# Branch B of a hybrid decoder layer: which marks free its buffers, and two buffers for each recurrent gate

## The reference, cut to what matters

```python
u = conv_b + sum(xpad[:, j:j + T] * conv_w[j] for j in range(CONV_W))
r = sigmoid(blockdiag(u, ga_w) + ga_b)
ig = sigmoid(blockdiag(u, gx_w) + gx_b)
log_a = -LRU_C * r * softplus(-lam)
a = exp(log_a)
bterm = sqrt(-expm1(2 * log_a)) * (ig * u)
hs = scan(h[t] = a[t] * h[t-1] + bterm[t])
y = hs * silu(z)
return y, hs[:, -1], xpad[:, T:]
```

## Time and profile before

| | us |
|---|---|
| runs shown | 1821.83, 1827.86, 1829.33 (median 1827.86) |
| profiled execution, its own time | 1816.9 |
| its span | 1815.1 |
| TensorE busy | 1612.6 (89% of the span) |
| VectorE busy | 913.3 (50%) |
| ScalarE busy | 563.0 (31%) |
| GpSimd busy | 471.7 (26%) |
| stretch of branch B | about 1386 to 1542 of the span |
| stretch of the last stage | 1542 to 1815 |

### The profile page before, as it was taken

One profiled execution on the slowest core, in us unless ns is written; L12 is line 12 of the kernel. 1 busy time (PEld: TensorE's weight loads), 2 busy tenths in 40 slices (PEclk: granted clock), 3 DMA queues, 4 the chain that ended last, 5 costly groups with the idle time before them and its releaser, 6 DMA issues. The chain is left out here.

```text
span 1815.1 us, 30544 instructions
## 1 busy us (share of the span) xinstructions
PE 1612.6 (89%) x11996; PEld 1418.7 (78%) x11996; DVE 913.3 (50%) x1504; ACT 563.0 (31%) x1111; POOL 471.7 (26%) x461
## 2 busy tenths in 40 slices
PE   7899988888886899999989898888899886999697
PEld 3789965666665788887878898888899875999697
DVE  1660456666551222332224258758873465478576
ACT  0312135544441322222212243625442574001100
POOL 2021101000012111211020366757662130234400
PEclk9899999999998999999999999999999998999899
DMA  9311120000004444334240401202132010644321
GB/s 306 129 48 48 25 83 1 1 1 1 1 2 117 118 131 121 110 106 109 83 139 21 153 24 36 72 25 72 30 104 84 22 52 1 207 152 156 107 101 64
DMA packets 162433, 143.48 MB, mean 79 GB/s; under 512 B 50902, under 2 KB 152306, under 8 KB 161394
## 3 DMA queue, kind: packets, MB, share of 16 engines
q1 hardware_dynamic: 153298, 127.79, 23.4%
q10 hardware_dynamic: 8992, 13.74, 2.2%
HBM read 116.21 MB, written 29.40 MB: 80 GB/s over the span
## 5 line engine op out<-in xcount | busy, mean ns | idle before, releaser
L1009 PE MATMUL ps<-w_hi,h_hi 128*128 128x256 f32 x792 | 228.6, 289 | 19.0 <-DVE h_lo L2522 13.6
L1009 PE MATMUL ps<-w_lo,h_hi 128*128 128x256 f32 x792 | 224.0, 283 | 0.0
L1009 PE MATMUL ps<-w_hi,h_lo 128*128 128x256 f32 x792 | 223.8, 283 | 0.0
L1009 PE MATMUL ps<-h_hi,w_hi 128*128 128x344 f32 x648 | 215.7, 333 | 8.9 <-DVE aq L2364 3.5
L1009 PE MATMUL ps<-h_lo,w_hi 128*128 128x344 f32 x648 | 209.4, 323 | 0.0
L1009 PE MATMUL ps<-h_hi,w_lo 128*128 128x344 f32 x648 | 209.0, 323 | 0.0
L1009 PEld LDWEIGHTS ps<-w_hi,h_hi 128*128 128x128 f32 x792 | 151.0, 191 | 21.1 <-issue 14.5
L1009 PE MATMUL ps<-h_hi,wg_hi 128*128 128x344 f32 x432 | 146.1, 338 | 14.0 <-ACT gate_stage L1780 13.1
L900 POOL CAST w_hi<-w_raw 128x1024 fp32r<-128x1024 f32 (+1 forms) x50 | 53.5, 1070 | 387.0 <-DMA w_raw<-in_w_in 163.3
L1009 PEld LDWEIGHTS ps<-w_lo,h_hi 128*128 128x128 f32 x792 | 151.1, 191 | 0.0
L1009 PEld LDWEIGHTS ps<-w_hi,h_lo 128*128 128x128 f32 x792 | 151.0, 191 | 0.0
(11 more groups left out here) (437 smaller groups left out, 3549.1 us busy)
## 6 DMA issues: line engine op xcount, KB each, us to landing
w_raw<-in_w_in SPq DMA_DIRECT2D x46, 512.0 KB, 4.9
sgm<-gate_spill SPq DMA_DIRECT2D x22, 516.0 KB, 6.0
gate_spill<-gate_stage ACTq DMA_DIRECT2D x54, 172.0 KB, 2.4
w_raw<-in_w_in SPq DMA_DIRECT2D x34, 256.0 KB, 4.3
adw<-in_ada_w SPq DMA_DIRECT2D x8, 1024.0 KB, 11.3
pgc<-in_cache_nsa_kv SPq DMA_DIRECT2D x128, 64.0 KB, 2.4
pg<-in_cache_nsa_kv SPq DMA_DIRECT2D x64, 128.0 KB
w_raw<-in_w_branch SPq DMA_DIRECT2D x12, 512.0 KB, 4.4
```

The source lines that it names most:

```text
L1009: last = mm(out, lhsT=l, rhs=r, start=(i == 0 and j == 0), stop=(i == n - 1 and j == 2))
```

## The change

- BR and BI get two buffers each (BR of the even blocks lies where a branch A buffer was, which is also the place of SGM[0] of the merge gates).
- ScalarE waits with BXP for u_ready (the convolution of two blocks before) instead of b_done; with the gate tiles for b_done of two blocks before; a new mark b_scan, given by the scan, frees BA and BT, and ScalarE waits for it before the exponential; BZ now waits for b_done of two blocks before, and so does SGM[0] at j = 4.
- OCO gets four columns, one for each block. The two copies from BXP go to the start of `b_conv`; the two from BHS come right after the scan.
- y is made in BZ instead of BA.

```diff
--- before.py
+++ after.py
@@ -459,13 +459,13 @@
     BXP = sb("bxp", o_, [2, 8 + 3 + T]); o_ += 2 * 1040
     BZ = sb("bz", o_, [2, TC]); o_ += 2 * TC
     BU = sb("bu", o_, [2, TC]); o_ += 2 * TC
-    BR = sb("br", o_, [TC]); o_ += TC
-    BI = sb("bi", o_, [TC]); o_ += TC
+    BR = [sb("br_even", O_CS, [TC]), sb("br_odd", o_, [TC])]; o_ += TC
+    BI = [sb("bi%d" % i, o_ + TC * i, [TC]) for i in range(2)]; o_ += 2 * TC
     BA = sb("ba", o_, [TC]); o_ += TC
     BT = sb("bt", o_, [TC]); o_ += TC
     BHS = sb("bhs", o_, [TC]); o_ += TC
     GWB = sb("gwb", o_, [2, 2, P]); o_ += 512
-    OCO = sb("oco", o_, [2, 32]); o_ += 64
+    OCO = sb("oco", o_, [4, 32]); o_ += 128
     OCR = sb("ocr", o_, [4, P], parts=32); o_ += 512
     assert o_ <= END, o_ - END
 
@@ -1563,7 +1563,7 @@
         def columns_out(j):
 
             pe.wait_ge(e("oc_cols"), j + 1)
-            nc.tensor.transpose(ps[0:20, 6, P * j:P * j + P], OCO[:, j % 2, 0:20], ID).then_inc(e("oc_rows"), 1)
+            nc.tensor.transpose(ps[0:20, 6, P * j:P * j + P], OCO[:, j, 0:20], ID).then_inc(e("oc_rows"), 1)
 
         for j in range(5):
             if j < 4:
@@ -1974,7 +1974,7 @@
                         if j == 0:
                             act.wait_ge(e("a_free"), 4)
                         if j >= 2:
-                            act.wait_ge(e("b_done"), j - 1)
+                            act.wait_ge(e("u_ready"), j - 1)
 
                         st(A(BXP[:, j % 2, 0:8], ps[:, b, 0:8], CP))
                         st(A(BXP[:, j % 2, 11:3 + CH], ps[:, b, 8:CH], CP), act3.free)
@@ -1983,18 +1983,21 @@
                 st.mark(e("bx_ready"))
             if j:
                 jj = j - 1
-                if jj:
-                    act.wait_ge(e("b_done"), jj)
-                for x, dst in ((0, BR), (1, BI)):
+                gr = BR[jj % 2]
+                if jj >= 2:
+                    act.wait_ge(e("b_done"), jj - 1)
+                for x, dst in ((0, gr), (1, BI[jj % 2])):
                     for c in range(3):
                         b = ta.take(act)
                         st(A(dst[:, CH * c:CH * c + CH], ps[:, 3 + b, 0:CH], ACT.Sigmoid, bias=PRM[:, 48 + 4 * x + jj:49 + 4 * x + jj]), ta.free)
 
-                st(A(BA, BR, ACT.Exp, scale=C8[:, jj:jj + 1]))
-                st(A(BT, BR, ACT.Tanh, scale=C8[:, 4 + jj:5 + jj]))
-
-                st(A(BR, BT, ACT.Ln, bias=1.0))
-                st(A(BR, BR, ACT.Exp, scale=-1.0), e("b_at"))
+                if jj:
+                    act.wait_ge(e("b_scan"), jj)
+                st(A(BA, gr, ACT.Exp, scale=C8[:, jj:jj + 1]))
+                st(A(BT, gr, ACT.Tanh, scale=C8[:, 4 + jj:5 + jj]))
+
+                st(A(gr, BT, ACT.Ln, bias=1.0))
+                st(A(gr, gr, ACT.Exp, scale=-1.0), e("b_at"))
 
             def b_gate(x):
                 for c in range(3):
@@ -2002,15 +2005,18 @@
                     st(A(SGM[x][:, CH * c:CH * c + CH], ps[:, b, 0:CH], ACT.Tanh, scale=0.5), act3.free)
 
             if j == 4:
+                act.wait_ge(e("b_done"), 3)
                 b_gate(0)
             if j < 4:
+                if j >= 2:
+                    act.wait_ge(e("b_done"), j - 1)
                 for c in range(3):
                     b = act3.take(act)
                     st(A(BZ[:, j % 2, CH * c:CH * c + CH], ps[:, b, 0:CH], CP), act3.free)
             if j:
                 act.wait_ge(e("b_om"), jj + 1)
                 st(A(BT, BT, ACT.Sqrt, scale=2.0))
-                st(A(BR, BZ[:, jj % 2, :], ACT.Sigmoid), e("b_sq"))
+                st(A(gr, BZ[:, jj % 2, :], ACT.Sigmoid), e("b_sq"))
             if j == 4:
                 b_gate(1)
 
@@ -2452,6 +2458,8 @@
             cb = PRM[:, 44 + j:45 + j]
             v.wait_ge(e("bx_ready"), j + 1)
             xp, us, up = BXP[:, s, 8:11 + T], BU[:, s, 0:NS], BU[:, s, NS:TC]
+            st(cp(OCO[:, j, 0:8], BXP[:, s, 0:8]))
+            st(cp(OCO[:, j, 8:11], BXP[:, s, 8 + T:11 + T]))
             st(ts(up, xp[:, 0:T], cw[0], cb, MUL, ADD))
             for i in (1, 2, 3):
                 st(stt(up, in0=xp[:, i:i + T], scalar=cw[i], in1=up, op0=MUL, op1=ADD))
@@ -2468,23 +2476,21 @@
             s = j % 2
             v.wait_ge(e("b_at"), j + 1)
 
-            st(tt(BT, BT, BR, MUL), e("b_om"))
-            st(tt(BI, BI, BU[:, s], MUL))
+            gr, gi, y = BR[s], BI[s], BZ[:, s]
+            st(tt(BT, BT, gr, MUL), e("b_om"))
+            st(tt(gi, gi, BU[:, s], MUL))
             st(tt(BHS[:, 0:NS], BA[:, 0:NS], CST[:, j, 24:32], MUL))
             v.wait_ge(e("b_sq"), j + 1)
-            st(tt(BI, BI, BT, MUL))
-            st(tt(BHS[:, 0:NS], BHS[:, 0:NS], BI[:, 0:NS], ADD))
-            st(V.tensor_tensor_scan(BHS[:, NS:TC], BA[:, NS:TC], BI[:, NS:TC], 0.0, MUL, ADD))
-            st(tt(BZ[:, s], BZ[:, s], BR, MUL))
-            st(tt(BA, BHS, BZ[:, s], MUL))
-            st(cp(YH[0][:, j], BA))
-            st(tt(YH[1][:, j], BA, YH[0][:, j].bitcast(F32), SUB))
-
-            oc = OCO[:, s]
-            st(cp(oc[:, 0:8], BXP[:, s, 0:8]))
-            st(cp(oc[:, 8:11], BXP[:, s, 8 + T:11 + T]))
+            st(tt(gi, gi, BT, MUL))
+            st(tt(BHS[:, 0:NS], BHS[:, 0:NS], gi[:, 0:NS], ADD))
+            st(V.tensor_tensor_scan(BHS[:, NS:TC], BA[:, NS:TC], gi[:, NS:TC], 0.0, MUL, ADD), e("b_scan"))
+            oc = OCO[:, j]
             st(cp(oc[:, 11:12], BHS[:, TC - 1:TC]))
             st(cp(oc[:, 12:20], BHS[:, 0:8]))
+            st(tt(y, y, gr, MUL))
+            st(tt(y, BHS, y, MUL))
+            st(cp(YH[0][:, j], y))
+            st(tt(YH[1][:, j], y, YH[0][:, j].bitcast(F32), SUB))
             if j:
                 b_rows(j - 1)
             st.mark(e("oc_cols"))
```

## The result

| | runs | median us | lowest to highest |
|---|---|---|---|
| before | 4 | 1828.59 | 1821.83 to 1829.56 |
| changed | 4 | 1807.60 | 1799.90 to 1812.99 |

The changed kernel takes 0.9891 of the time before (95% interval 0.9856 to 0.9925), 19.9 us less by the ratio and 21.0 us less by the medians. The forecast was 1806.9 us.

What follows compares the result with a forecast made beforehand. TensorE bound it, idling in branch B because b_done released several buffers together. Between 19.0 and 22.4 us won, 21 was taken off the median 1827.86, giving 1806.9 us, range 1798 to 1819.

Steps and rivals of the forecast that it cites:

- Second set: Branch B gate products, j=2: ScalarE reads banks directly, six products take about 3.3 us; 5.3 us won.
- New wait for weights: TensorE before x3: weights loaded behind b_done and split by GpSimd are ready at 1458.5, a wait of about 1 us.
- Third set: Gate products, j=3: the set takes 3.3 us, z3 begins at 1473.3 against 1481.59; 8.3 us won so far.
- Fourth set: Gate products, j=4: TensorE's wait falls from 15.11 to 3.9 us; BG begins at 1492.7, or 1494.2 at half clock.
- The scan: VectorE before ScalarE's exponential at j=4: b_scan at 1494.3, with ScalarE then waiting for TensorE at BG's last bank.
- The y products: End of branch B: y products begin at 1519.9 instead of 1542.26, 22.4 us earlier; 19.0 at the low end.
- mishap: Half clock after the fourth wait, 2.3 us together, or GpSimd holding BT*gr, 1.1 us on the path; one taken, not both.
- y in z's place: Recurrence tail: with the four-column OCO it changes no duration, so nothing beyond the 0.41 us from the copies.
- rival 2: Last stage, 1650 to 1700 us: its idleness grows and gives back 14.4 us, leaving 6.6 us won, 1821; chance 0.08.
- Rival 1: ScalarE-VectorE ring over single BA, BT, BHS still binds if GpSimd holds fall on it: 9.4 us lost, 1816; chance 0.10.
- rival 3: Kernel slower: chip grants half clock in dense stretches; 60 us of it gives 1867, 31 us gives 1838; chance 0.04.
- 4: The rival that something else in ScalarE's order holds the fourth set: at most 8.3 us won, 1819.5; chance 0.05.

Runs made afterwards that it cites:

- e9: e7's kernel with the last stage's first split once its buffer is free, the second after oc_done; 106.60 us from first gate set to first y product.
- e4: Changed kernel with ScalarE waiting for b_done instead of b_scan before the exponential; 114.33 us from first gate set to first y product, against 108.77.
- e1: Changed kernel with both old b_done waits back, for x and gate banks; 128.14 us from first gate set to first y product, run of 1833.47.
- e7: Changed kernel with the edits of e5 and e6, and unit BG loaded early too; 106.62 us from first gate set to first y product.
- e10: Changed kernel with GpSimd waiting in branch A for x_ready of the same head before its long operations; 1794.77 us, 0.9826 of before.
- e12: Kernel before with only the branch A wait of e10; 1816.64 us, 0.9931 of the kernel before.
- e6: Changed kernel with GpSimd waiting for block 2's b_scan before splitting the last stage's first weights; 112.08 us from first gate set to first y product.
- e2: Changed kernel with only x waiting for b_done again; 114.27 us from first gate set to first y product, against 108.77.
- e3: Changed kernel with only the gate banks waiting for b_done of the block just before; 123.96 us from first gate set to first y product.
- e5: Changed kernel with the fourth x group's weights loaded ahead of SyncE's wait; 106.99 us from first gate set to first y product, against 108.77.
- e8: e7's kernel with 27 matmuls of the first y products made during TensorE's wait; 376.1 us from first gate set to end, run of 1799.50.
- e11: Edits of e9 and e10 with the partial products of e8; 1790.21 us, 0.9789 of the kernel before.

## Why the prediction was right, point by point

I put the changed kernel's times back by the 12.95 us of branch A, so that they stand on the prediction's clock. x3 is the x group of block 3, z2 the z group of block 2.

- **Second set.** Forecast: z2 begins at 1445.4. Measured 1458.27-12.95 = 1445.3. Right to a tenth, including that six products with ScalarE beside them take 3.2 us.
- **New wait for weights.** Forecast about 1 us, x3 at 1458.6. Measured 1.73 us between records and 2.0 from z2's transpose, x3 at 1459.2. GpSimd's second subtraction took 3.21 us here instead of 2.40, held by VectorE; the sum had no term for that direction of the lock.
- **Third set.** Forecast: z3 at 1473.3. Measured 1475.4, 2.1 us late. 0.6 is the weights. The rest is the step "x3 takes 11.42 us", which failed: behind a pause of only 2.0 us the products ran on at full clock for 1.4 us and then at half clock for about 3, and x3 took 12.97 us. The window over x3 in the changed kernel, in the columns named with e9, shows a mean granted clock of 0.87:

```profile
1472.10:1485.10 13.00, 12.94 (x72) 12.94 (x73) 9.96 (x12) 4.28 (x6) 0.00 (x1) 0.87 0.00 1
```

- **Fourth set.** Forecast: a wait of 3.9 us, BG at 1492.7 or 1494.2. Measured 3.66 us at full clock throughout, and 1507.61-12.95 = 1494.7, late by the third set's 2.1 us alone.
- **The scan.** Forecast 1494.3, measured 1511.15-12.95 = 1498.2: 2.05 us from the third set and 1.89 from the hold by GpSimd. I had priced that hold, and then called it hidden behind BG's group. That step was wrong: ScalarE came to the merge gates' banks at 1519.66 when the last was about ready, TensorE waited 0.81 us for one of them, and about 1 us of the hold reached the end.
- **The y products.** Forecast 22.4 us earlier without mishap, 19.0 with all of them, 21 taken. Measured 19.13. That this lies between the two bounds is luck in part, for neither of the mishaps that the lower bound was made of came: the fourth wait was followed by full clock, and BT*gr of block 2 took 1.23 us. Three others took 3.2 us of the 22.4: 0.6 for the weights and 1.5 for x3, where the sum had no such terms, and about 1.1 for the hold of gi*BT, which it had called hidden.
- **y in z's place.** Forecast: nothing beyond 0.41 us. This step failed, though the sum did not: the chain used b_scan, which exists only because y no longer needs BA. e4 puts it at 5.56 us.
- **The last stage.** Forecast: moves as a block. It took 1.48 us more in this profile; over the profiles of before, changed, e1 to e7, e9, e10 and e12 it lies between 272.8 and 274.3 us, with e12, which does not have the change, at 273.8. So this is its own spread, and rival 2 falls.
- **The signs of being wrong.** Of the three that were named, one came: b_scan ended a wait longer than 2 us at j = 4, 2.35 us. It is the hold of gi*BT again, without which about 0.5 us would be left of that wait (e6 has 0.46). The fourth wait (3.66 us against a limit of 8) and the stretch behind the first y product (1.48 us longer against 3) stayed clear.
- **Rivals 1, 3 and 4.** e2 and e3 show the waits gone for the reason given, so 4 falls. Rival 1's ring did bind for 2.35 us at one place, not for 9. For rival 3, from 1584 to 1644 us the granted clock was 1.00 in the changed kernel as it was in the kernel before. The same view of that window in the changed kernel:

```profile
1584.00:1644.00 60.00, 58.17 (x363) 56.90 (x362) 46.04 (x60) 0.00 (x0) 25.17 (x14) 1.00 0.42 144
```

- **The median.** 1806.9 forecast, 1807.6 measured. Part of this is luck: four runs that spread over 13 us for reasons of branch A could as well have given 1803 or 1811. The profiled execution, forecast at 1795.9, took 1812.15 us, most of the difference in branch A. The e10 and e12 pair gives 19.3 us and the profiles 19.1, and so the 21 us were 1.7 to 1.9 us too large as a size, less than these medians can resolve. The stated range, too, is wider than its own working: 19 to 22.4 us widened by 4 us either side is 1801.5 to 1812.9, not 1798 to 1819. The measured median lies in both.

## What to carry to other kernels

When one mark at the tail of a stage frees several buffers, ask of each what its last reader is; a mark at that reader, or a second buffer, takes the tail off the cycle, and it can depend on where a result is written (y in BA or in BZ) whether the early mark is possible at all. Price each such step at the place where its wait ends last: here 15.2, 5.5 and 5.6 us, by three experiments that put one old wait back each. And before trusting a comparison of two spans, cut both at common instructions: a stretch that the edit doesn't touch had moved by 13 us, and the wait that steadied it was worth about two thirds of the change itself.

## What the runs showed of the hardware that I had not expected

- **VectorE and GpSimd exclude each other, in both directions, and one wait that settles who comes first was worth about 12 us.** VectorE's 1.23 us products took up to 3.33 us beside GpSimd's subtractions, and GpSimd's 2.40 us subtraction took 3.21 beside VectorE's work. The Trainium skill (SBUF — State Buffer, section "Who interferes with whom") states that a VectorE instruction with two SBUF inputs and a GpSimd instruction that reads SBUF take a shared pair of ports in turn, for a whole instruction. The traces agree. In e5 a scan belongs to them too: GpSimd's subtraction that began at 1503.69, 0.03 us behind VectorE's scan of 2.29 us, took 4.44 us. In head 2 of branch A the order of the two hung on a DMA landing 0.8 us earlier or later, and the earlier landing was the slower case.
- **The same wait is followed by either clock.** The fourth set waits 3.66 us in nine of these kernels and 3.67 in e2. The six records behind it span 2.01 us in the changed kernel and in e6 (full clock), 3.19 to 3.51 in e10, e4 and e2, and 3.81 in e5, e7, e8, e9 and e11 (half clock). A pause of 2.0 us ahead of x3 was followed by half clock in the changed kernel and in e4 and e10, and took 1.55 us each time. What decides it, these runs do not show.
- **Moving work out of one hold put it into another.** e6 cured the slow product and lost more on three others. e9 put the splits where VectorE was idle and no operation on y was slow, and then TensorE at half clock was the bound; whether that can be had back was not tried.
